# Layer 2's attention: diagonal chunks exponentiated in two parts around a zero corner, in place of an added mask

## The reference, cut to what matters

```python
s = jnp.einsum('bqhd,bkhd->bhqk', qi, k, preferred_element_type=jnp.float32) * scale
visible = ci[:, None] >= chunk_id[None, :]
s = jnp.where(visible[None, None], s, NEG)
p = jax.nn.softmax(s, axis=-1)
return jnp.einsum('bhqk,bkhd->bqhd', p.astype(v.dtype), v)
```

## Time and profile before

| | us |
|---|---|
| median of 3 runs (3781.49 to 3787.76) | 3786.57 |
| the profiled execution's own time | 3779.09 |
| its span, first to last instruction | 3777.3 |
| TensorE busy over the span | 3527.0 (93%) |
| VectorE busy | 1758.2 (47%) |
| ScalarE busy | 1118.6 (30%) |
| GpSimd busy | 1073.8 (28%) |

### The profile page before, as it was taken

One profiled execution on the slowest core, in us unless ns is written; L12 is line 12 of the kernel. 1 busy time (PEld: TensorE's weight loads), 2 busy tenths in 40 slices (PEclk: granted clock), 3 DMA queues, 4 the chain that ended last, 5 costly groups with the idle time before them and its releaser, 6 DMA issues.

```text
span 3777.3 us, 39362 instructions
## 1 busy us (share of the span) xinstructions
PE 3527.0 (93%) x16368; PEld 2824.1 (75%) x16368; DVE 1758.2 (47%) x1817; ACT 1118.6 (30%) x1427; POOL 1073.8 (28%) x1144
## 2 busy tenths in 40 slices
PE   9988889999999999999898999999989899999997
PEld 6655667888887688555498989988966777777776
DVE  4666553222223678566456545544563323443522
ACT  3333342111112522334432111111233422222432
POOL 3111344232323333000023334433323222111243
PEclk9999999999999999899899999999999999999999
DMA  3000211111111211000021111111112111000232
GB/s 119 23 28 23 98 59 62 45 51 45 47 49 51 79 67 40 12 6 6 6 82 43 40 51 45 46 46 50 45 52 77 51 67 45 28 23 34 73 128 95
DMA packets 56249, 192.22 MB, mean 51 GB/s; under 512 B 6900, under 2 KB 7284, under 8 KB 55560
## 3 DMA queue, kind: packets, MB, share of 16 engines
q1 hardware_dynamic: 56072, 189.71, 14.5%
HBM read 172.83 MB, written 16.86 MB: 50 GB/s over the span
## 4 chain that ended last, share of the span: by engine, by line
PE 80%; DVE 12%; ACT 5%; issue 2%; DMA 1%; POOL 0%; DVEq 0%; ACTq 0%; SPq 0%; POOLq 0%
PE psum L263 21%; PE psum L265 20%; PE psum L264 20%; PE psum L136 14%; DVE work L96 3%; DVE mix L105 2%; DVE res L96 1%; PE psum L296 1%; PE psum L298 1%; PE psum L297 1%; DVE res L105 1%; ACT L124 1%; DVE u_padded L96 1%; DVE work L114 1%; ACT res L124 1%
## 5 line engine op out<-in xcount | busy, mean ns | idle before, releaser
L96 POOL TENSOR_TENSOR w_lo<-w_raw,w_hi 128x256 fp32r<-128x256 f32 x1140 | 1073.6, 972 | 2668.6 <-ACT w_hi L129 2668.3
L263 PE MATMUL psum<-x_hi,w_hi 128*128 128x512 f32 (+2 forms) x3336 | 1256.7, 377 | 37.7 <-DVE mix L96 7.2
L264 PE MATMUL psum<-x_lo,w_hi 128*128 128x512 f32 (+2 forms) x3336 | 1209.7, 363 | 0.0
L265 PE MATMUL psum<-x_hi,w_lo 128*128 128x512 f32 (+2 forms) x3336 | 1206.8, 362 | 0.0
L129 ACT CAST w_hi<-w_raw 128x1024 fp32r<-128x1024 f32 x285 | 298.2, 1048 | 1637.0 <-PE psum L265 1539.1
L263 PEld LDWEIGHTS psum<-x_hi,w_hi 128*128 128x128 f32 x3336 | 634.1, 190 | 149.4 <-issue 42.1
L264 PEld LDWEIGHTS psum<-x_lo,w_hi 128*128 128x128 f32 x3336 | 635.0, 190 | 93.0 <-issue 20.3
L265 PEld LDWEIGHTS psum<-x_hi,w_lo 128*128 128x128 f32 x3336 | 633.0, 190 | 80.9
L263 PE MATMUL psum<-h_hi,w_hi 128*128 128x512 f32 x848 | 338.4, 399 | 15.5 <-issue 9.0
L265 PE MATMUL psum<-h_hi,w_lo 128*128 128x512 f32 x848 | 336.2, 396 | 0.0
L264 PE MATMUL psum<-h_lo,w_hi 128*128 128x512 f32 x848 | 333.7, 394 | 0.0
(11 more groups left out here) (281 smaller groups left out, 3604.9 us busy)
## 6 DMA issues: line engine op xcount, KB each, us to landing
w_raw<-w_dram SPq DMA_DIRECT2D x285, 512.0 KB, 3.2
res<-spill SPq DMA_DIRECT2D x4, 1044.0 KB, 9.2
res<-x_dram SPq DMA_DIRECT2D x8, 512.0 KB, 9.1
res<-x_dram SPq DMA_DIRECT2D x4, 1024.0 KB, 8.2
spill<-res SPq DMA_DIRECT2D x1, 4096.0 KB, 13.9
spill_a<-mix SPq DMA_DIRECT2D x8, 512.0 KB, 2.6
res<-spill_a SPq DMA_DIRECT2D x8, 512.0 KB, 4.8
x_plain<-spill SPq DMA_DIRECT2D x4, 1024.0 KB, 11.1
```

Of the source, the lines that this page charges most:

```text
L96: self.mark(self.e.tensor_tensor(out, a, b, op), inc)
L263: t.e.matmul(out, whi, xhi, start=k == 0, stop=False, skip_group_check=True)
L264: t.e.matmul(out, whi, xlo, start=False, stop=False, skip_group_check=True)
L265: ins = t.e.matmul(out, wlo, xhi, start=False, stop=last_k, skip_group_check=True)
```

## The change

Diagonal chunks get no mask product. Their second score pass ends the group and carries the semaphore. ACT takes their exponential in two instructions: keys 0 to 63 for the first 64 columns, then all 128 keys for the rest, so that the hidden corner (keys 64 to 127, columns 0 to 63) is never written. They go to three buffers of their own, `diagonal_probs`, whose corners DVE sets to zero once, with three memsets more before the first head; `pe_weigh` reads these buffers over their full width, zeros and all. The other chunks keep `probs`. The waits of `act_exp` are unchanged; the first score product waits for 15 counts of `heads_set` instead of 12. The small mask of `pe_score` stays.

```diff
--- before.py
+++ after.py
@@ -1362,6 +1362,7 @@
         self.k_rot, self.rope_t = self.M[6], self.M[7]
         res, work = core.res[:, :, :].rearrange("p a b -> p (a b)"), work[:, :, :].rearrange("p a b -> p (a b)")
         self.probs = [res[:, 400 * i:400 * i + 400] for i in range(4)]
+        self.diagonal_probs = [res[:, 2400 + 400 * i:2800 + 400 * i] for i in range(3)]
         self.o_raw = [res[:, 1600 + 400 * i:2000 + 400 * i] for i in range(2)]
         self.v_t = res[:, 3672:8352].rearrange("p (n h c) -> p n h c", n=9, h=H2)
         self.rot_parts = work[:, 2688:3036]
@@ -1631,7 +1632,7 @@
         if n == 0:
             for m in range(9):
                 t.wait_ge(*self.k.products["v2", m].freed)
-            t.wait_ge(self.heads_set, 12)
+            t.wait_ge(self.heads_set, 15)
         for m in range(3):
             t.wait_ge(*self.k.products["keys", h // 2, m].freed)
         t.wait_ge(self.q_rounded, h + 1)
@@ -1676,11 +1677,16 @@
         self.chunk_ring.append(r)
         t.wait_ge(*self.ring_freed[self.rows[h, p]])
         k0, out = self.first_key(b), self.k.ps[rows, bank, 0:m]
-        diagonal = b > 0 and b in PIECES2[p][2]
-        products = [(out, self.keys[h % 3][0:QK + 1, k0:k0 + rows.stop], self.q_t[h % 2][0:QK + 1, q0:q0 + m], True, not diagonal)]
-        if diagonal:
-            products.append((out[:, 0:P], self.mask[0:1, P:2 * P], self.mask[0:1, 0:P], False, True))
-        t.mm(products, self.filled)
+        t.mm([(out, self.keys[h % 3][0:QK + 1, k0:k0 + rows.stop], self.q_t[h % 2][0:QK + 1, q0:q0 + m], True, True)], self.filled)
+
+    def diagonal(self, c):
+
+        b = lambda x: CHUNKS2[x][2] > 0 and CHUNKS2[x][2] in PIECES2[CHUNKS2[x][1]][2]
+        return sum(b(x) for x in range(c)) if b(c) else None
+
+    def probs_of(self, c):
+        n = self.diagonal(c)
+        return self.probs[c % 4] if n is None else self.diagonal_probs[n % 3]
 
     def pe_weigh(self, t, c):
 
@@ -1690,7 +1696,7 @@
         t.wait_ge(*self.ring_freed[self.chunk_ring[c]])
         if b == 0:
             t.wait_ge(self.o_copied, 3 * h + p)
-        t.mm([(self.k.ps[0:65, 6, c0:c0 + m], self.v_t[rows, b, h, :], self.probs[c % 4][rows, 0:m], b == 0, b == PIECES2[p][2][-1])], self.weighed)
+        t.mm([(self.k.ps[0:65, 6, c0:c0 + m], self.v_t[rows, b, h, :], self.probs_of(c)[rows, 0:m], b == 0, b == PIECES2[p][2][-1])], self.weighed)
 
     def ended(self, c):
 
@@ -1871,7 +1877,12 @@
         r, (rows, _, m) = self.chunk_ring[c], self.chunk(c)
         a.wait_ge(self.filled, r + 1)
         a.wait_ge(self.weighed, c - 3)
-        a.act(self.probs[c % 4][rows, 0:m], self.k.ps[rows, 3 + r % 3, 0:m], ACT.Exp, inc=self.copied)
+        probs, scores = self.probs_of(c), self.k.ps[:, 3 + r % 3, :]
+        if self.diagonal(c) is None:
+            a.act(probs[rows, 0:m], scores[rows, 0:m], ACT.Exp, inc=self.copied)
+        else:
+            a.act(probs[0:64, 0:64], scores[0:64, 0:64], ACT.Exp)
+            a.act(probs[:, 64:m], scores[:, 64:m], ACT.Exp, inc=self.copied)
 
     def act_head_copy(self, a, c):
         u = self.ended(c)
@@ -2060,6 +2071,8 @@
         v.settle()
         v.memset(mask[:, 0:64], -1e30, inc=self.heads_set)
         v.memset(mask[:, P + 64:2 * P], 1.0, inc=self.heads_set)
+        for probs in self.diagonal_probs:
+            v.memset(probs[64:P, 0:64], 0.0, inc=self.heads_set)
         v.memset(self.mix[:, 4:8, META + S:WIDE], 0.0)
 
     def dve_max(self, v, n):
```

## The result

The changed kernel takes 3755.69 us, the median of 4 runs (3751.83 to 3758.68). The kernel before takes 3786.72 in the same comparison (4 runs, 3781.49 to 3787.76). The ratio is 0.9919, interval 0.9903 to 0.9935: 31 us faster, where the prediction had 20 and its range ended at 3758.

What follows compares the result with a forecast made beforehand. TensorE, busy 93% of the span, was taken as the bound. 64 less 11 masks at 0.40 us gave 21.2, less 0.8 and 0.6: 19.8 us off 3786.57, forecast 3766.6 us, range 3758 to 3778.

Steps and rivals of the forecast that it cites:

- The mask at 0.40 us: On TensorE at diagonal chunks, each of 64 large masks costs 0.40 us, from 0.39 before a weighing and 0.43 before scores.
- Far above what 128 columns stream: On TensorE, a mask's 0.39 us before a weighing was said to exceed by far the streaming of its 128 columns.
- The streaming rival: On TensorE, a mask costs only its 128 columns, 0.053 us: 3.4 us saved, 3783 us; chance 0.06.
- The split at 0.05 us on ACT, hidden: On ACT, each of 64 second exponentials adds 0.05 us (bounds 0 and 0.168), covered by the chunk's about 0.34 us earlier start.
- Memsets at nothing: Before the first head, three DVE memsets of 0.112 us each cost nothing, standing before DVE idle time; uncovered, 0.3 us once.
- 11 masks returned to waits: In heads 1, 3 and 5 (3 masks), head 5 (4) and head 6 (4), longer TensorE waits take back the savings.
- Heads 5 and 6 "only 1 to 2" us shorter each: Heads 5 and 6 shorten by only 1 to 2 us each, with longer layer norm waits; heads 1 to 4 by 2.5 to 3.
- the sum: Over the attention, 53 masks at 0.40 us, less 0.8 for an exponential on the path and 0.6 for DVE: 19.8 us.
- DVE takes over: In the second half of every head DVE becomes the bound and 8 us go: gain 12, 3775 us; chance 0.14.
- a denser TensorE might be held at the lower level for a third longer: In the attention, 19 us more at 1.2 GHz cost at most 9 us: gain 11, 3776 us; chance 0.05.
- the 56 us at 1.2 GHz: In the attention window of 350 us, granted clock 0.92 was read as 56 us at the lower clock level.
- TensorE's waits for ACT's `res`: In the profile after, growth of these waits was named as a sign that the prediction is wrong; no size given.

Runs made afterwards that it cites:

- e1: The changed kernel again with no edit, beside the kernel before on the same chip: 3758.41 us, ratio 0.9919.
- e5: The kernel before with the large mask's product cut from 128 columns to 16: 3780.7 us, ratio 0.9988.
- e6: The kernel before with the large mask's product 97 rows high instead of one, the added rows zero: 3766.63 us, ratio 0.9954.
- e2: The kernel before without the 64 large masks, exponential whole in the old buffers, corner not hidden: 3752.57 us, ratio 0.9911.
- e4: The changed kernel with the large mask product put back, so only the split exponential differs from before: 3784.51 us, ratio 0.9997.
- e7: The changed kernel with the large mask put back everywhere except in heads 5 and 6: 3776.04 us, ratio 0.9981.
- e8: The changed kernel with the small mask products of the row maxima left out too: 3744.24 us, ratio 0.9895.
- e10: The changed kernel, unedited, one profiled execution: 3757.97 us.
- e9: The kernel before, unedited, one profiled execution: 3791.32 us.
- e12: The changed kernel, unedited, a second single profiled execution: 3759.57 us.
- e3: The kernel before with each large mask product issued twice, 64 products more: 3787.53 us, ratio 1.0004.
- e11: The kernel before, unedited, a second single profiled execution: 3781.87 us.

## Why the prediction was right about the mask and too small in all

- **The mask at 0.40 us.** Right. In the changed kernel's profile the chunk's step is 0.44 for 0.78 and the weighing 0.43 for 0.48. Heads 1 and 3 at full clock lost 2.7 us each. In e1, TensorE is busy 22.8 us less over 64 masks, 0.36 each, at nearly the clock of before.
- **"Far above what 128 columns stream."** Right, and e5 and e6 show what it is: 0.05 us goes with the columns and 0.29 with the single row. The streaming rival (3783) is out.
- **The split at 0.05 us on ACT, hidden.** Right: 0.54 for 0.49, and 0.43 for 0.38; e2 and e4 find nothing of it in the time.
- **Memsets at nothing.** Three of 112 ns, before the same wait. TensorE's first score product still waits 3.5 us for ACT's `x_hi` at line 129, by the list of waits of the changed kernel below.
- **11 masks returned to waits.** Right in the places, wrong in the number. 0.23 became 0.49, 2.10 became 3.06, 2.22 became 2.48. TensorE's idle time rose by 4.1 us in e1, near the 11 x 0.40 = 4.4 that were taken off, but the low clock in heads 5 and 6 (0.86 for 0.90) makes TensorE busier there and hides a part of the growth.
- **Heads 5 and 6 "only 1 to 2" us shorter each.** Wrong, and the smaller of the two steps that failed: their window is 0.8 us longer, or 0.2 shorter in e7. All its masks went back to waits, where the sum had 8 of 16 doing so. That makes the sum some 2 us too large.
- **DVE takes over (3775).** Did not happen for this change: TensorE's waits for the softmax shifts of line 111 are 5.4 us, where they were 4.9. It is the next bound, as e8 shows. TensorE's waits for ACT's `res` (2.2 us) didn't grow by more than 0.1.
- **The clock: "a denser TensorE might be held at the lower level for a third longer", gain 11.** This is the step that failed. The clock entered only as a rival that takes something back, with 0.05 of the chances, and the sum was made as if the 56 us at 1.2 GHz of the earlier trace rows stayed. They went down, not up: from 66 us in the attention to 48 in the usual execution of the change. The rival also priced a microsecond at the lower level at no more than half; that part was right.

What the lower level costs depends on the stage. In heads 0 to 4, e1 against the first profile of the change prices it: 8.2 us for 42 - 20 = 22 us, 0.37 each. In head 7, before against e7 gives 0.43, and in heads 5 and 6, e10 gives nothing. From this, as an estimate for the first pair of profiles (us):

| stage | before to after | of it the clock | of it the masks |
|---|---|---|---|
| heads 0 to 4, 43 masks | 22.4 | (36 - 20) x 0.37 = 5.9 | 16.5, 0.38 each |
| heads 5 and 6, 15 masks | -0.8 | 0 | -0.8 |
| head 7, 6 masks | 5.6 | 8.6 x 0.43 = 3.7 | 1.9, 0.32 each |
| attention | 27.2 | 9.6 | 17.6 |

So the masks gave 17.6 us where the sum had 19.8, and the clock some 10 us where the sum had nothing.

The waits of TensorE in the attention (waited for: us, times, longest), of before and then of the changed kernel:

```profile
PE psum L136 <- DVE softmax_shift_columns L111: 4.9, 3, 2.2
...
PE psum L136 <- ACT res L124: 2.1, 2, 1.0
```

```profile
PE psum L136 <- DVE softmax_shift_columns L111: 5.4, 3, 2.5
...
PE psum L136 <- ACT x_hi L129: 3.5, 1, 3.5
...
PE psum L136 <- ACT res L124: 2.2, 3, 1.0
```

That settles the attention. For the whole kernel there is the granted clock of every run, to three digits. Behind the first comparison, whose runs of before have none on record, the kernel before has 49 (23, 23, and 3 with e9 to e12): mean 3784.6 us at a mean clock of 0.9631, 280 us at the lower level. The changed kernel has 11 in all: mean 3756.6 at 0.9653, 261 us. Within the 23 runs of before on either chip, each microsecond more at the lower level goes with 0.38 and 0.37 us more time (the slope of a straight line through them). So of 28.0 us between the means, (280 - 261) x 0.37 = 7 are the clock, and 21 are left. Runs of the same clock say it without a slope: at 0.965 nine of before have a mean of 3779.3 us (3778.05 to 3780.82) and six of the change 3758.4 (3756.31 to 3759.57), 20.9 us apart. The masks' 17.6 in the table lie below this because the low clock also moved within the attention: out of head 7, where it costs 0.43, into heads 5 and 6, where it costs nothing.

This also explains the first pair of profiles. Both have 0.965 over the whole kernel, so they compare at an equal clock, and 20.4 us is what the change gives there. Inside them the low clock had only moved: 18 us less in the attention, and some 17 more in the rest, which took 6.8 us longer. That the profiled 3758.68 met the forecast of 3759.3 is luck in this sense: the forecast left the clock as it was, and in this one pair it was. Over more profiles the rest of the kernel scatters from 3414.8 (e7) to 3429.9 (e9), with no difference in its mean: 3422.7 over three profiles of before, 3422.3 over four of the change.

The forecast of the median failed by the clock. It was 3786.57 less 19.8 (that is 3766.8; the prediction writes 3766.6), and the medians of the change were 3755.69 and 3758.41. The medians of before over 23 runs each were 3783.89 and 3784.59, so the 3786.57 on which the prediction stood may have been 2 us high, if the chips are alike. The remaining 3 us between 3755.69 and 3758.41 lie within the 8 us over which the runs of e1 spread.

What stays open is why the clock is granted more fully. One place can be named. The first 30 us of the attention, in the kernel before and in e6, whose masks are all there, 97 rows high:

```profile
1527.84:1557.84 30.00, 27.68 (x71) 14.73 (x71) 9.71 (x15) 5.50 (x11) 0.00 (x0) 0.54 0.00 0
```

```profile
1527.57:1557.57 30.00, 27.61 (x87) 16.02 (x87) 11.25 (x18) 7.65 (x15) 0.00 (x0) 0.66 0.00 0
```

The seven executions with the large one-row masks in head 0 have 0.50 to 0.54 there (before, e3, e4, e5, e7, e9, e11). Of the seven without, five have 0.66 (the first of the change, e2, e6, e10, e12), e8 has 0.61 and e1 0.55. So the earlier rise goes with the stalls being gone, and not with the masks being gone. But one execution of the changed program didn't have it, and no run shows why.

In head 4 the same wait for DVE's `work` at line 96 stands in three profiles. Before, TensorE's timeline and the window behind it:

```profile
1715.69 0.66 PE L296 MATMUL psum<-x_hi,w_hi 128*128 128x348 f32 x1 [1.17 <-DVE work L96]
```

```profile
1715.60:1722.40 6.80, 6.71 (x17) 3.62 (x18) 1.74 (x4) 0.71 (x2) 0.00 (x0) 0.50 0.00 0
```

Of the changed kernel, where the same wait is 1.16 us long, the whole of head 4:

```profile
1695.83:1731.04 35.21, 33.62 (x158) 20.32 (x158) 28.57 (x37) 14.02 (x39) 5.80 (x4) 1.00 0.05 16
```

In e1, the same program, the stretch behind that wait:

```profile
1704.60:1711.40 6.80, 6.80 (x17) 3.65 (x17) 2.26 (x5) 0.92 (x2) 0.00 (x0) 0.50 0.00 0
```

A wait of 1.17 us was followed by 6.8 us at 1.2 GHz twice, and one of 1.16 by none once. This fall stands behind a wait of TensorE, but whether the wait is followed by one changes between executions of one program.

## What to carry to other kernels

Price a small product between large ones by the distance between the starts of its neighbours, with and without it, and never by its columns: here one row cost seven times its streaming, and widening it to 97 rows made the kernel 18 us faster without any other change. Where a stage of the trace has a granted clock below 1.00, write the clock as a term of the sum with bounds on both sides. In this kernel a microsecond at the lower level cost about 0.4 us where TensorE was the bound, and nothing to 0.2 where it waited for others. Take more than one profile before calling the first one's clock the kernel's, and compare runs of equal clock. Where a stage goes at the pace of waits for other engines, ask whether all its masks are returned: in heads 5 and 6 all were, where the sum had half. When a time is met, look at its parts: here the profiled total (3758.68 for 3759.3) and the attention of e7 (3.2 for 3) were both met by terms that had moved.

## What the runs showed of the hardware that I had not expected

- A product with one row between products of 97 and 128 rows costs 0.34 us, the same product with 97 rows 0.05 (e6). The one-row weight load starts 0.53 us behind the start of its chunk, the 97-row load 0.22. A second one-row product right behind the first costs 0.11 (e3), and 16 columns instead of 128 save 0.05 (e5).
- The recorded length of the mask's product hides this. Its least and its median in the earlier trace rows are 292 and 321 ns over both forms of the one-row mask, and 0.41 us in the timeline of e6, where the product is the cheap one. Only distances between starts tell the cost.
- One program had an attention of 334.2 us in one execution and 342.7 in another, with nothing but the granted clock between them (0.93 and 0.90). In heads 5 and 6 the clock cost nothing: 107.81 us at 0.87 in the first profile of the change and 107.84 at 0.84 in e10.
